# Decoder trunk on one core: first norm's row vectors loaded at the layer's start, its row pass placed behind expert 0's product

## What is computed

```python
x = layer_norm(DEEPNORM_ALPHA * x + heads_out @ w_out[l], ln1_g[l], ln1_b[l])   # called x1 here
ffn = grouped_moe(x, router_w, router_b, exp_w_gate[l], exp_w_up[l], exp_w_down[l])
x = layer_norm(DEEPNORM_ALPHA * x + ffn, ln2_g[l], ln2_b[l])
# grouped_moe: each token is sent to 2 of 16 experts; of expert e
he = jax.nn.silu(h @ w_gate[e]) * (h @ w_up[e])
out = out + gate[:, e:e + 1] * (he @ w_down[e])
```

## Time and profile before

| | |
|---|---|
| three runs | 864.36, 864.5 and 866.28 us, median 864.5 |
| profiled execution | 866.47 us, its span 864.6 us |
| PE busy | 800.7 us, 93% of the span |
| DVE, ACT, POOL busy | 315.2, 180.6, 26.0 us |
| moved by DMA | 245.87 MB |

### The profile page before, as it was taken

One profiled execution on the slowest core, in us unless ns is written; L12 is line 12 of the kernel. 1 busy time (PEld: TensorE's weight loads), 2 busy tenths in 40 slices (PEclk: granted clock), 3 DMA queues, 4 the chain that ended last, 5 costly groups with the idle time before them and its releaser, 6 DMA issues. The chain is left out here.

```text
span 864.6 us, 13075 instructions
## 1 busy us (share of the span) xinstructions
PE 800.7 (93%) x5493; PEld 436.2 (50%) x5493; DVE 315.2 (36%) x646; ACT 180.6 (21%) x371; POOL 26.0 (3%) x103
## 2 busy tenths in 40 slices
PE   9999999988999999989799999999799999999883
PEld 8888666545333333323288876664453333333331
DVE  1296445565111111111343964373741111111115
ACT  1142322333001110000222223232330011100001
POOL 7100000000000000000000000000000000000000
PEclk9999999998999999999989999999999999999998
DMA  9945200397899999999945532014969999999992
GB/s 281 322 150 181 99 2 2 134 425 267 303 417 420 421 421 419 422 422 420 398 143 190 186 108 99 2 68 161 423 255 346 423 420 421 420 421 423 420 421 98
DMA packets 55252, 245.87 MB, mean 284 GB/s; under 512 B 8356, under 2 KB 13328, under 8 KB 30608
## 3 DMA queue, kind: packets, MB, share of 16 engines
q1 hardware_dynamic: 53840, 240.20, 70.3%
q0 software_dynamic: 1344, 4.72, 1.7%
HBM read 243.85 MB, written 1.05 MB: 283 GB/s over the span
## 5 line engine op out<-in xcount | busy, mean ns | idle before, releaser
L552 PE MATMUL bank<-ring,xg 128*64 128x512 f32 x544 | 127.0, 610 | 6.3 <-DMA ring<-in_exp_w_up 3.9
L1054 PE MATMUL bank<-x_cm,ring 128*128 128x256 f32 x576 | 127.8, 383 | 0.9 <-ACT x_cm L2020 0.9
L1054 PEld LDWEIGHTS bank<-x_cm,ring 128*128 128x128 f32 x576 | 110.3, 192 | 17.4 <-ACT x_cm L2020 1.2
L552 PE MATMUL bank<-ring_more,xg 128*64 128x512 f32 x416 | 96.4, 605 | 5.7 <-DMA ring_more<-in_exp_w_up 5.7
L787 DVE TENSOR_TENSOR y_lo<-bank,y_hi 128x512 fp32r<-128x512 f32 x32 | 22.1, 692 | 196.4 <-ACT y_hi L718 187.4
L552 PEld LDWEIGHTS bank<-ring,xg 128*64 128x64 f32 x544 | 38.7, 139 | 76.2 <-issue 74.0
L772 DVE TENSOR_SCALAR x_cm<-bank,g_col 128x512 f32<-128x512 f32 x32 | 24.0, 751 | 107.6 <-PE bank L552 105.1
L552 PEld LDWEIGHTS bank<-ring_more,xg 128*64 128x64 f32 x416 | 30.4, 138 | 58.8 <-issue 57.7
L586 PE MATMUL bank<-ring_more,x_cm 128*64 128x512 f32 x256 | 58.2, 596 | 1.9 <-issue 1.9
L586 PE MATMUL bank<-ring,x_cm 128*64 128x512 f32 x256 | 57.8, 594 | 1.1 <-DVE g_col L763 1.1
L1061 PE MATMUL bank<-ring,x_cm 128*128 128x512 f32 x128 | 57.7, 599 | 0.0
(11 more groups left out here) (381 smaller groups left out, 873.9 us busy)
## 6 DMA issues: line engine op xcount, KB each, us to landing
ring<-in_exp_w_gate SPq DMA_DIRECT2D x36, 1024.0 KB, 17.1
ring<-in_exp_w_up SPq DMA_DIRECT2D x36, 1024.0 KB, 18.8
ring_more<-in_exp_w_down SPq DMA_DIRECT2D x32, 1024.0 KB, 18.3
ring<-in_exp_w_down SPq DMA_DIRECT2D x32, 1024.0 KB, 15.4
ring_more<-in_exp_w_gate SPq DMA_DIRECT2D x26, 1024.0 KB, 17.2
ring_more<-in_exp_w_up SPq DMA_DIRECT2D x26, 1024.0 KB, 18.9
ring<-in_w_in SPq DMA_DIRECT2D x24, 1024.0 KB, 8.1
ring<-in_w_out SPq DMA_DIRECT2D x8, 1024.0 KB, 6.3
```

The source lines that it names most:

```text
L552: m = T.matmul(b[half_of(n, i), :], xg[g][:, 4 * h + k, cols], w[:, k, :], start=(h == 0 and k == 0), stop=(h == 1 and k == 3))
L1054: m = T.matmul(out_, w[:, k, c:c + n], x_cm[:, k, :], start=(k == 0), stop=(k == KD - 1))
```

## The change

ln1's gain and bias get a place of their own. `ln_gain` is new memory. `ln_bias` is allocated and given back at once, so that `y_hi` and `y_lo`, allocated next, lie in the same bytes; they were allocated among the experts' tiles before. Therefore `y_high(0)` now waits for `v_x1`. POOL issues the two loads (2 x 512 KB) as the layer begins, behind the two `gn_vec` loads; in layer 1 these wait for `v_x2` of layer 0. The row pass of x1 moves from in front of DVE's branch to behind `product(0)`. `hidden(0, 1)` waits for `s_first` block by block and not for all of it ahead.

```diff
@@ allocation of memory
+        ln_gain = sb("ln_gain", [P, D])
+        with nc.sbuf_tensor("ln_bias", [P, D], F32) as ln_bias:
+            pass
+        F32R = mybir.dt.float32r
+        y_hi = sb("y_hi", [P, BCOL], F32R)
+        y_lo = sb("y_lo", [P, BCOL], F32R)
...
         mixers.close()
-        F32R = mybir.dt.float32r
         ring_more = sb("ring_more", [P, MORE, 4, BCOL])
-        ln_rows = [x_cm[:].rearrange("p k s -> p (k s)").rearrange("p (a d) -> p a d", a=2),
-                   ring_more[:, 0].rearrange("p k n -> p (k n)").rearrange("p (a d) -> p a d", a=2)]
+        ln2_rows = ring_more[:, 0].rearrange("p k n -> p (k n)").rearrange("p (a d) -> p a d", a=2)
+        ln_rows = [[ln_gain[:], ln_bias[:]], [ln2_rows[:, i] for i in range(2)]]
...
-        y_hi = sb("y_hi", [P, BCOL], F32R)
-        y_lo = sb("y_lo", [P, BCOL], F32R)
@@ hidden(n, h), tensor engine
                 for k in range(4):
+                    if n == 0 and h == 1 and rounds == 1:
+                        pe.wait_ge(*done("s_first", l, 4 + k + 1))
                     for i, w in enumerate(ws):
@@ experts_t, tensor engine
             inc(m, "t_pos")
-            if rounds == 1:
-                pe.wait_ge(*done("s_first", l))
             gathered = GU
@@ y_high(n), scalar engine
                 if n:
                     act.wait_ge(*at("t_scat", n))
+                else:
+                    act.wait_ge(*done("v_x1", l))
@@ experts_v, vector engine
-        def experts_v(dve, l, rounds):
+        def experts_v(dve, l, rounds, rows_of_x1):
...
                     product(n)
+                if n == 0:
+                    for j in range(TT):
+                        rows_of_x1(j)
                 if n == N - 2:
@@ gpsimd block, for each layer
                     if which:
-                        pool.wait_ge(*done("v_sel", l))
-                        for i, name in enumerate(("ln1_g", "ln1_b")):
-                            pool.dma_start(ln_rows[0][:, i, :], t[name][l].partition_broadcast(P)).then_inc(ln_loaded.sem, 16)
                         last = max(n for n, q in enumerate(loads) if q[0] == l and slot_of[n] == NSLOT)
...
                     if which == 0:
                         for i, name in enumerate(("rwkv_ln_g", "rwkv_ln_b")):
...
+                        for i, name in enumerate(("ln1_g", "ln1_b")):
+                            pool.dma_start(ln_rows[0][i], t[name][l].partition_broadcast(P)).then_inc(ln_loaded.sem, 16)
@@ vector block, after the routing
                 do(V.tensor_tensor(gate[:], gate[:], wide(rms_s[:, :, 0], NE), ALU.mult))
-                for j in range(TT):
-                    rows_of_x1(j)
                 chained = c.n
```

More of the change, by code:

```diff
@@ L996, in _ @@
                         for i, name in enumerate(("ln2_g", "ln2_b")):
-                            pool.dma_start(ln_rows[1][:, i, :], t[name][l].partition_broadcast(P)).then_inc(ln_loaded.sem, 16)
+                            pool.dma_start(ln_rows[1][i], t[name][l].partition_broadcast(P)).then_inc(ln_loaded.sem, 16)
                     if which == 0:
@@ L1580, in affine_rows @@
                     dve.wait_ge(ln_loaded.sem, 64 * l + 32 * (which + 1))
-                    do(V.tensor_tensor(x_tm[:, j], x_tm[:, j], ln_rows[which][:, 0], ALU.mult))
-                    inc(V.tensor_tensor(x_tm[:, j], x_tm[:, j], ln_rows[which][:, 1], ALU.add), "v_x1" if which == 0 else "v_x2")
+                    do(V.tensor_tensor(x_tm[:, j], x_tm[:, j], ln_rows[which][0], ALU.mult))
+                    inc(V.tensor_tensor(x_tm[:, j], x_tm[:, j], ln_rows[which][1], ALU.add), "v_x1" if which == 0 else "v_x2")
                 def out_half(j, hf):
@@ L1587, in out_half @@
                     do(V.scalar_tensor_tensor(out=x_tm[:, j, cs], in0=x_tm[:, j, cs] if j else bank[hf][:], scalar=bn2[:, j, 0:1],
-                                              in1=ln_rows[1][:, 0, cs], op0=ALU.subtract, op1=ALU.mult))
+                                              in1=ln_rows[1][0][:, cs], op0=ALU.subtract, op1=ALU.mult))
                     ins = V.scalar_tensor_tensor(out=x_tm[:, j, cs], in0=x_tm[:, j, cs], scalar=bn2[:, j, 1:2],
-                                                 in1=ln_rows[1][:, 1, cs], op0=ALU.mult, op1=ALU.add)
+                                                 in1=ln_rows[1][1][:, cs], op0=ALU.mult, op1=ALU.add)
                     ins.then_inc(out_ready, 1)
@@ L1992, in experts_and_norm @@
                     c.n = chained
-                    experts_v(dve, l, rounds)
+                    experts_v(dve, l, rounds, rows_of_x1)
                     layer_norm(l, 1)
```

## The result

| | before | changed |
|---|---|---|
| median of the runs | 864.67 us (6 runs, 861.27 to 866.28) | 858.26 us (6 runs, 856.3 to 859.35) |
| profiled execution, span | 864.6 us | 857.5 us |

The ratio is 0.9927, with a 95% interval of 0.9911 to 0.9943: 6.3 us faster, where 4.8 us were forecast, and the time lies in the stated range. By the interval the gain lies between 4.9 and 7.7 us. In the runs beside the experiments, on three chips, the kernel before had medians of 865.5 to 866.0 us (17 to 23 runs); the changed kernel has no runs beside those, so the 7 us and more that one gets from them is not a comparison side by side.

The account below looks back on a forecast made before the run. Experts were held bound by PE and DMA, both hanging on how early PE gets through expert 0. Terms 2.54 + 1.59 + 0.68 = 4.81 us less: profiled 866.47 becomes 861.7, median 864.5 becomes 859.7; range 857.9 to 862.3.

Parts of the forecast that it names:

- The bound: Experts of each layer: a microsecond won at expert 0 moves slot releases, transfer backlog and end by a microsecond.
- Rival 2: Experts' weight stream takes the gain back, PE waiting longer at the end: time 864.5, chance 0.07.
- Layer 0's terms: Before and in `hidden(0, 1)`: 2.54 us of PE's wait for DVE and 1.59 us of low clock saved.
- The signs: Layer 0, if right: gates start without a wait at about 208.1, SP's next issue moves to about 212.6.
- Rival 1: Layer 0's `hidden(0, 1)`: the clock falls all the same, 1.59 us stay, time 861.3, chance 0.15.
- Layer 1's term: Ahead of `hidden(0, 1)`: 0.29 us of wait for DVE and 0.39 us for `s_first`, gain 0.68 us.
- rival 5: Another stretch of low clock, such as layer 1's gathering, shrinks by 1.6 us more: 858.1, chance 0.05.
- with the row pass gone from in front of the branch: Layer 0: DVE reaches its branch at 201.45, PE asks some 6 us later; gain 2.54 us.
- The block-wise wait: Before `hidden(0, 1)`: waiting by block carries 0.6 us of layer 0's 2.54 and 0.39 us in layer 1.
- The cover: Behind `product(0)`: the moved row pass ends with about 0.9 us left over, so it costs 0.
- Rival 3: The row pass delays `scatter(0)` through `y_high(0)`'s new wait: 4.95 us slower, 869.5, chance 0.04.
- rival 4: Layer 0's first projections: weights come late by 2.6 us at about 37, time 862.3, chance 0.03.

Follow-up runs that it names:

- experiment 7: The change with the row pass made longer by one or three DVE instructions that change no value: 859.56 us with one, 862.93 us with three.
- experiment 3: The change with the row pass of x1 put back in front of DVE's branch, early loads and block-wise wait kept: 857.93 us.
- experiment 4: The kernel before with only the early loads in their own place, row pass and whole wait for `s_first` as before: 861.29 us.
- experiment 6: The change with ln1's loads issued behind `v_sel` again, but into their own place: 860.05 us.
- experiment 9: The filled pair: idle PE products between the two tiles' turns and ahead of the selection; kernel before so filled 865.91 us, change so filled 858.2 us.
- experiment 5: The kernel before with the block-wise wait for `s_first` alone: 864.97 us.
- experiment 8: Idle PE products at three places, one being layer 1's entry; kernel before so filled 870.32 us, change so filled 862.85 us.

## Why the prediction was right, and where it was not

**The bound.** Right for what is won at expert 0: it went through to the end of layer 0 undiminished (3.39 and 3.38 us). Over all profiles, what lies between SP's issue and layer 0's last scatter takes 207.6 to 208.6 us where the vectors are still loaded into `x_cm` and 206.5 to 208.6 in the change and its like, and what lies between the issue in layer 1 and the end takes 221.9 to 222.3 and 221.1 to 222.4. PE's waits for weights grew by 1.0 us over both layers (9.6 to 10.6) in the first pair of profiles, not by what was won. Rival 2 is refuted. One piece later it does not hold in full: of the 8.5 us lost ahead of `down(1)` in both layers (experiment 7, three more instructions), some 5.5 reach the layers' ends.

**Layer 0's terms.** The signs came late by the clock of the gathering: the gates start at 208.94 (forecast 208.1), SP issues at 213.31 (212.6). The 2.54 us of wait and the 1.59 us of clock behind it are right as a pair for an execution in which PE gathers at full clock: the filled pair shows 17.84 against 13.80 us, 4.04 us, where the two terms make 4.13. For one in which it gathers at 1.2 GHz the same edit gives 16.51 against 15.36, 1.15 us. The summed profile was of the first kind in layer 0 and the changed kernel's of the second. Rival 1 is refuted: the fall behind the wait is gone in every profile in which the wait is gone or down to 1.1 us. The change's own profile could not show this for a gathering at full clock; experiments 3, 4, 6 and 9 do.

**Layer 1's term, the one that was mis-sized.** I put 0.68 us there "since PE's gathering came later", and did not ask why it came later: the earlier trace rows had its clock, 0.50 at 629. In that state the term is right (16.20 against 15.35, 0.85 us). At full clock it is as large as layer 0's: 17.70 against 13.79 us, 3.91 us. The sum took one draw of the clock for each layer as if it were the kernel's. By the stages the gain lies between about 2 us (both slow) and 8 us (both fast), and the 6.3 us of the medians lie in that span. How often each draw comes in the unprofiled runs isn't shown, so this accounts for the surplus over 4.8 us without proving it; the kernels filled at two places have the same medians as the unfilled ones (experiment 9). (Block 7 is needed three quarters of the way into the products and not two thirds, as the fourth of four; nothing hangs on it.)

**The range.** That 858.26 us lies in it is partly luck. The low end, 857.9, came from rival 5 and not from the terms, and of the 7.1 us between the two profiles only 3.5 are what the terms are about.

**What holds DVE.** The step "with the row pass gone from in front of the branch" named the wrong part of the edit. The loads alone do it (experiments 3 and 4), and so, by the stages, does the move without early loads (experiment 6). The 4.50 us of idle time for the vectors, in the earlier trace rows beside the pass, were the cost; the pass's own 4.88 us fit before PE asks.

**The block-wise wait.** I had 0.6 us of the 2.54 on it in layer 0 and 0.39 us in layer 1. Measured it is 0.8 to 0.9 us in each layer by the stages, and 3.2 to 3.4 us by the medians (861.41 to 858.26, 861.29 to 857.93), which did not run side by side. Half of that I can place; the other half stays open, and is not far above what two medians of one program differ by (0.9 us). It was worth nothing alone (experiment 5), as its place behind DVE's wait says.

**The new place, and the start.** The cover was forecast at 0.9 us and is 0.99 us. The early loads delayed nothing that I can find: PE waited for no weights before 195 in either kernel, and the first layer's projections, take 27.79 us as before:

```profile
17.14 27.79 PE L1063 MATMUL bank<-x_cm,ring 128*128 128x256 f32 x128
```

Rival 3 needs one more DVE instruction to begin, rival 4 did not happen.

**Rival 5** came true for a part. Of the 7.1 us between the two spans, 3.5 us are stages and about 2 us are the shorter low clock in layer 1's first products. I can't show that the change causes it: over the experiments' profiles, kernels with the early loads and kernels without them both had from 3.4 to 10 us of low clock there.

## What to carry to other kernels

When an engine stands in front of others because of one instruction, look at what that instruction waited for before moving it: a small transfer issued earlier can do the same with less edit. Two waits in series must be taken out together: the one that comes second showed nothing clear of the scatter by itself here and 3 us once the first was gone, and their order in the profile says which hides which. And where the clock of the stretch ahead of a wait differs between executions or layers, the wait's length in one profile is not its price: take the stage from a fixed event to a fixed event, at both clocks.

## What was not expected of the hardware

PE leaves its branch and skips the code of the four rounds, and its next product starts only some 5.5 us after the last scatter. The profile puts that idle time down to `bn` on ACT, but in the changed kernel ACT had written its rows by 426.64 and the turns began at 428.19:

```profile
425.19 1.45 ACT L2245 ACTIVATE x_rows<-bank,neg_mean,bn 128x512 f32<-128x512 f32 x2
...
428.19 3.36 PE L1037 MATMUL bank<-ident,x_rows 128*128 128x128 f32 x16 [5.58 <-ACT bn L2164]
```

Products that wait for nothing began no earlier (experiment 8: 5.52 us). So the delay is PE's own and not its data's; what PE does in it no run here shows.
